# Retention heads one, two and three begin two, two and one slots later in a two-layer mixer kernel

## The chip, the cores and the metric

The kernel runs on one core of a Trainium2 chip. The metric is the device time of one execution in microseconds (us); the times shown are those of whole executions, and the profile comes from one further execution.

## What is computed

The reference is a stack of two layers over 512 positions of width 1024, followed by a norm. A layer normalises x, multiplies it by one wide matrix w_in, and feeds pieces of the result to four branches: a short convolution, a sparse attention (compressed, selected and window parts), a retention and a pooling. Gates weigh the branches, w_o adds them to x, and a gated feed-forward part follows. The change concerns the retention, cut here to what matters:

```
q = rotary(zq, pos, dk); k = rotary(zk, pos, dk) * dk ** -0.5     # 4 heads of 128
def step(R, inp):                                                 # chunks of 128 positions
    scores = einsum('bhnd,bhmd->bhnm', qc, kc) * intra            # decay, causal
    inner  = einsum('bhnm,bhme->bhne', scores, vc)
    ...
mu = mean(o); var = mean(square(o - mu))
o = ((o - mu) * rsqrt(var + EPS)) * gn_g
return o * silu(zg)
```

The kernel does a head as one decayed causal product over the 512 positions, in four row blocks of keys.

## The kernel before, in words

Everything is transposed: features on the 128 partitions, the 512 positions along the free dimension. Every weight matrix is cut into groups of 128 output features by 1024 input features (512 KB). SyncE (SP) loads the groups in order into a ring of three; ScalarE (ACT) copies a group to its high part `w_hi` (L431, two groups ahead of the matmul, once the group before has been multiplied); GpSimd (POOL) subtracts to make the low part `w_lo` in two halves (L415); TensorE (PE) multiplies a group in 24 matmuls of 512 columns (L1107 to L1109: high by high, high by low, low by high, for eight chunks). VectorE (DVE) takes the finished product out of one of two accumulators with the step `take` (L650), which also frees that accumulator; PE may be two products ahead of it at most.

After twelve groups for the attention inputs (A) come 32 groups (B) that make the inputs of retention, convolution and pooling. Their order is the table `B_TILES`: head h of the retention has its four tiles rq, rk, rv, rg at the places 0, 16, 20 and 24 on. Each B product is cut in four quarters of six matmuls, and between the quarters PE does small pieces of the branches. The table `SIDE` says which piece stands in which of the 128 slots (slot n is quarter n mod 4 of product n div 4). PE, DVE and ACT each walk through the same table in order, and each does its own part of every piece, so that a place in the table is a place in three queues. No engine passes a step that waits.

For head h, with n0 = `RET_SLOT[h]`, the loop over the heads puts these pieces:

```
for _m in range(QT):
    SIDE[_n0 + _m].append(("ret_scores", _h, _m))
    SIDE[_n0 + _m + 1].append(("ret_values", _h, _m))
SIDE[_n0 + 5].append(("ret_gate", _h))
SIDE[_n0 + 6].append(("ret_var", _h))
SIDE[_n0 + 7].append(("ret_inverse", _h))
SIDE[RET_SLOT[_h] + (8, 8, 8, 12)[_h]].append(("ret_end", _h))
SIDE[RET_SLOT[_h] + (14, 12, 12, 14)[_h]].append(("ret_split", _h))
SIDE[4 * (RET0[_h] + 3) + 3].append(("ret_turn", _h))
SIDE[4 * (_b + 2) + 1 + _k].append(("rotate", B_TILES[_b], _k))
```

The last two do not depend on `RET_SLOT`: the transposes of rv (`ret_turn`) and the rotary steps (`rotate`) stay by their tiles.

What each piece is:

- `ret_scores` (PE L1316, rk by rq into a bank `s`; DVE L872 multiplies it by the decay into `pr`). Block 0 waits for the rotated rk. `ret_values` (PE L1326, rv by pr into a bank `o`) waits for that multiplication.
- with the last `ret_values` ACT squares and copies the result (L527, L528). `ret_gate`: ACT tanh of rg (L522), DVE L886. `ret_var`: PE L1333 sums the squares over partitions, ACT takes the square root (L532), DVE inverts one half (L892); `ret_inverse`: DVE inverts the other (L895). tanh and root each need a table load on ACT. `ret_end` (DVE L906, L908) scales, `ret_split` (DVE L899, L900) writes the high and low parts.
- `ret_turn`: PE transposes rv_T (L1191, waits for the take of rv), DVE L879, L880.
- `rotate`: ACT issues two DMAs that swap the halves of rq or rk into `rot` (L459, L460), at the start of the product after that tile, when the tile's take is done; DVE L690, L692 in one slot and L694 in the next.
- `pool` (PE L1342, DVE L918, L919), and for ACT a load of the decay table of a head (L498) at products 14, 18, 22 and 26.

On ACT, the start of every B product is in this order: the copy `w_hi`, the two swap DMAs, the decay DMA; the pieces of that product's four slots follow.

After B come eight rounds that multiply gates and branches, the product with w_o, and the feed-forward part; the change touches nothing there.

Of the kernel before, what the change touches and what calls it, by code (L numbers as in the profile page):

```python
# [69 lines left out]
A_TILES = ["k_cmp", "v_cmp", "k_slc", "k_win", "v_slc", "v_win", "q0", "q1", "q2", "q3", "gate", "pad"]  # L70
RET0 = [0, 16, 20, 24]
SC0 = [4, 7, 10, 29]
RET_SLOT = [68, 80, 96, 112]
POOL0 = [28, 13, 14, 15]
POOL_SLOT = [127, 85, 101, 117]
B_TILES = [None] * B_GROUPS
# [29 lines left out]
for _h in range(RH):  # L106
    _n0 = RET_SLOT[_h]
    for _m in range(QT):
# [6 lines left out]
for _h in range(RH):  # L115
# [3 lines that stand above are left out]
# [1429 lines left out]
```

## Time and profile before

| | us |
|---|---|
| median of 3 runs (2152.16 to 2152.82) | 2152.51 |
| the profiled execution | 2152.31 |
| its span, first to last instruction | 2150.5 |
| mean granted TensorE clock over the span | 0.988 of full |
| chain of work that ended last: PE, DVE, issue | 91%, 6%, 2% |
| B slots 80 to 127 of layer 0, about | 310 to 408 |

The page gives the busy time of each engine, the chain of work that ended last (followed back from the last instruction to whatever released each step), and groups of instructions by line. A timeline lists instructions of one engine in order; the bracket at the end is the idle time of the engine just before, and who ended it. An x2 or x4 row stands for as many passes.

### The profile page before, as it was taken

The numbers are of one execution on the slowest core, as the hardware profiler recorded it, in microseconds if no ns is written. First come the engines' busy times: TensorE is split into PE (matmuls) and PEld (weight loads), VectorE is DVE, ScalarE is ACT, GpSimd is POOL, SyncE is SP. The second block draws the span as 40 slices with busy tenths as digits, with TensorE's granted clock in tenths as the row PEclk, the third lists the DMA queues.
The fourth block names the chain that finished last, engine by engine and source line by source line (L and its number), as shares of the span: only waits on it lengthen the run. The fifth ranks groups of instructions, "written<-read, shape, count | busy, mean of one in ns | idle before, by whom it ended". The sixth has DMA issues, their size and how long they took to land.

```text
span 2150.5 us, 32302 instructions
## 1 busy us (share of the span) xinstructions
PE 2086.4 (97%) x9834; PEld 1643.1 (76%) x9834; DVE 1227.3 (57%) x1856; ACT 659.8 (31%) x961; POOL 920.8 (43%) x676
## 2 busy tenths in 40 slices
PE   7999989999999999999999999999999999999997
PEld 5766667788888788888877666668888887888885
DVE  8656766622235888872157568565223278888513
ACT  3244423333332222222223445223233322222222
POOL 3422223444444555545534222234444454555552
PEclk9999999999999999999999999999999999999998
DMA  5311122222222222223232111222322232222332
GB/s 188 103 55 50 50 64 89 85 93 96 98 98 98 88 98 98 98 90 109 98 122 93 50 40 50 77 86 88 102 94 96 98 98 89 97 98 98 101 107 98
DMA packets 57131, 194.90 MB, mean 91 GB/s; under 512 B 6864, under 2 KB 7248, under 8 KB 56912
## 3 DMA queue, kind: packets, MB, share of 16 engines
q1 hardware_dynamic: 52272, 186.14, 26.1%
q10 hardware_dynamic: 4768, 7.61, 1.4%
q8 instruction: 50, 0.82, 0.2%
q14 instruction: 41, 0.34, 0.1%
HBM read 186.64 MB, written 2.10 MB: 88 GB/s over the span
## 4 chain that ended last, share of the span: by engine, by line
PE 91%; DVE 6%; issue 2%; ACT 0%; DMA 0%; DVEq 0%; ACTq 0%; SPq 0%
PE acc L1107 27%; PE acc L1109 27%; PE acc L1108 27%; PE o L1292 2%; PE s L1266 2%; PE t L1274 2%; PE o L1326 1%; PE s L1253 1%; PE s L1316 1%; PE s L1183 0%; PE t L1303 0%; DVE ssq L639 0%; DVE xg_lo L618 0%; PE s L1342 0%; DVE y_lo L900 0%
## 5 line engine op out<-in xcount | busy, mean ns | idle before, releaser
L415 POOL TENSOR_TENSOR w_lo<-w_raw,w_hi 128x512 fp32r<-128x512 f32 x672 | 920.6, 1390 | 1202.1 <-ACT w_hi L431 1190.4
L1107 PE MATMUL acc<-xg_hi,w_hi 128*128 128x512 f32 x1904 | 780.1, 410 | 18.4 <-DVE xg_lo L618 11.5
L1109 PE MATMUL acc<-xg_hi,w_lo 128*128 128x512 f32 x1904 | 748.9, 393 | 0.0
L1108 PE MATMUL acc<-xg_lo,w_hi 128*128 128x512 f32 x1904 | 748.0, 393 | 0.0
L431 ACT ACTIVATE w_hi<-w_raw 128x1024 fp32r<-128x1024 f32 x336 | 355.1, 1057 | 902.0 <-PE acc L1109 837.8
L1107 PEld LDWEIGHTS acc<-xg_hi,w_hi 128*128 128x128 f32 x1904 | 360.8, 190 | 127.3 <-issue 38.8
L1109 PEld LDWEIGHTS acc<-xg_hi,w_lo 128*128 128x128 f32 x1904 | 361.0, 190 | 77.8
L1108 PEld LDWEIGHTS acc<-xg_lo,w_hi 128*128 128x128 f32 x1904 | 361.7, 190 | 76.4 <-issue 6.9
L987 DVE TENSOR_TENSOR work<-acc,rstd 128x512 f32<-128x512 f32 x64 | 44.1, 690 | 256.1 <-PE acc L1109 256.1
L1107 PE MATMUL acc<-act_hi,w_hi 128*128 128x512 f32 x352 | 136.9, 389 | 0.0
L1108 PE MATMUL acc<-act_lo,w_hi 128*128 128x512 f32 x352 | 136.9, 389 | 0.0
L1109 PE MATMUL acc<-act_hi,w_lo 128*128 128x512 f32 x352 | 136.9, 389 | 0.0
L1081 DVE SCALAR_TENSOR_TENSOR x<-acc,x 128x512 f32 x16 | 11.1, 693 | 177.5 <-PE acc L1109 177.5
L993 DVE SCALAR_TENSOR_TENSOR work<-work,acc 128x512 f32<-128x512 f32 x64 | 44.0, 687 | 103.1 <-PE acc L1109 103.1
L1107 PE MATMUL acc<-y_hi,w_hi 128*128 128x512 f32 x256 | 99.6, 389 | 0.0
L1108 PE MATMUL acc<-y_lo,w_hi 128*128 128x512 f32 x256 | 99.6, 389 | 0.0
L1109 PE MATMUL acc<-y_hi,w_lo 128*128 128x512 f32 x256 | 99.6, 389 | 0.0
L566 ACT ACTIVATE work<-work 128x512 f32<-128x512 f32 x44 | 27.8, 632 | 186.4 <-DVE work L1036 186.4
L1108 PEld LDWEIGHTS acc<-act_lo,w_hi 128*128 128x128 f32 x352 | 66.1, 188 | 13.8
L1107 PEld LDWEIGHTS acc<-act_hi,w_hi 128*128 128x128 f32 x352 | 66.1, 188 | 13.7
L1109 PEld LDWEIGHTS acc<-act_hi,w_lo 128*128 128x128 f32 x352 | 66.1, 188 | 13.7
L842 DVE COPY pT<-t 128x128 f32<-128x128 f32 (+3 forms) x128 | 56.8, 486 | 28.3 <-PE t L1274 27.4
(190 smaller groups left out, 2231.1 us busy)
## 6 DMA issues: line engine op xcount, KB each, us to landing
w_raw<-weights_dram SPq DMA_DIRECT2D x339, 512.0 KB, 3.3
x<-xT_dram SPq DMA_DIRECT2D x8, 256.0 KB, 6.1
rot<-rq ACTq DMA_DIRECT2D x16, 128.0 KB
rot<-rk ACTq DMA_DIRECT2D x16, 128.0 KB
dec<-decay_dram ACTq DMA_DIRECT2D x8, 256.0 KB, 3.6
out_dram<-x SPq DMA_DIRECT2D x8, 256.0 KB, 2.2
con<-consts_dram SPq DMA_DIRECT2D x1, 1598.0 KB, 10.8
w1k<-w_dram SPq DMA_DIRECT2D x2, 512.0 KB, 9.3
```

Of the source, the lines that this page charges most:

```text
L415: nc.gpsimd.tensor_tensor(w_lo[:, k, part], w_raw[:, k, part], w_hi[:, k, part].bitcast(F32), ALU.subtract).then_inc(lo_ready, 1)
L431: nc.scalar.activation(w_hi[:, slot, :], w_raw[:, slot, :], ACT.Copy).then_inc(hi_ready, 1)
L566: nc.scalar.activation(work[:, 2, :], work[:, 1, :], ACT.Tanh, scale=0.5).then_inc(silu_ready, 1)
L842: t_end(ve.tensor_copy(pT[:, u % 2, 0:w], t_of(e)[:, 0:w]), e)
L987: ve.tensor_tensor(work[:, n, :], acc[n % 2][:, :], rstd[:, :], ALU.mult).then_inc(acc_free, 1)
L993: ve.scalar_tensor_tensor(out=work[:, n, :], in0=work[:, n, :], scalar=1.0, in1=acc[n % 2][:, :], op0=ALU.add, op1=ALU.mult).then_inc(acc_ ...
L1107: mm(tile, w_h, right_hi, start=first, stop=False)
L1108: mm(tile, w_h, right_lo, start=False, stop=False)
L1109: return mm(tile, w_l, right_hi, start=False, stop=last)
L1266: mm(b[:, 0:w], qT[r, h % 4, qi * P:(qi + 1) * P], kT[r, br, 0:w], start=True, stop=True).then_inc(s_done, 1)
L1274: ins = nc.tensor.transpose(b[:, k * P:(k + 1) * P], pr_of(u)[:, k * P:(k + 1) * P], ident)
L1292: ins = mm(o_bank[qi % 2][d, j * P:(j + 1) * P], v[:, d], p[:, half, :], start=(br == 0 and k == 0), stop=(br == 1 and k == qi + 1))
```

## The change

Heads one, two and three begin at the slots 82, 98 and 113 in place of 80, 96 and 112. All that is counted from `RET_SLOT` moves with them; `ret_turn`, `rotate`, `pool`, the tiles, the DMAs at the start of a product and head zero stay.

```diff
-RET_SLOT = [68, 80, 96, 112]
+RET_SLOT = [68, 82, 98, 113]
```

ACT, between the third and the fourth product after head one's scores (slots 85 to 88), before. L522 is the tanh of the gate, L532 the root, L431 the copy for the next weights, L459 and L460 the swap of rk of head two, L498 the decay of head two:

```order
L522 ACT_TABLE_LOAD
L522 ACTIVATE rg_t<-rg 128x512
L530 REGISTER_ALU
L532 ACT_TABLE_LOAD
L532 ACTIVATE pT<-s,con 128x512
L429 REGISTER_ALU
L430 REGISTER_ALU
L431 ACTIVATE w_hi<-w_raw 128x1024
L455 REGISTER_ALU
L457 REGISTER_ALU
L459 DMA rot<-rk 64x512
L460 DMA rot<-rk 64x512
```

and now:

```order
L522 ACTIVATE rg_t<-rg 128x512
L429 REGISTER_ALU
L430 REGISTER_ALU
L431 ACTIVATE w_hi<-w_raw 128x1024
L455 REGISTER_ALU
L457 REGISTER_ALU
L459 DMA rot<-rk 64x512
L460 DMA rot<-rk 64x512
L497 REGISTER_ALU
L498 DMA dec<-decay_dram 128x512
L530 REGISTER_ALU
L532 ACT_TABLE_LOAD
```

The root (L532, its table load and the activation after it) has moved from before the start of product 22 to behind it: behind the weight copy, the two swap DMAs and the decay DMA. The same holds for head two at product 26. For head three, gate and root stay in one product (29), as before.

DVE from the gate of head one to the take of rk of head two, before (L603 and the like are register work):

```order
L886 SCALAR_TENSOR_TENSOR rg<-rg_t,rg 128x512
L603 REGISTER_ALU
L655 REGISTER_ALU
L918 TENSOR_SCALAR y_hi_58<-s,vec 128x512
L603 REGISTER_ALU
L919 SCALAR_TENSOR_TENSOR y_lo_62<-s,vec,y_hi_58 128x512
L891 REGISTER_ALU
L892 RECIPROCAL pT<-pT 128x256
L603 REGISTER_ALU
L895 RECIPROCAL pT<-pT 128x256
L662 REGISTER_ALU
L649 REGISTER_ALU
```

and now:

```order
L886 SCALAR_TENSOR_TENSOR rg<-rg_t,rg 128x512
L603 REGISTER_ALU
L649 REGISTER_ALU
L650 TENSOR_TENSOR rk<-acc,rstd 128x512
L651 REGISTER_ALU
L891 REGISTER_ALU
L892 RECIPROCAL pT<-pT 128x256
L603 REGISTER_ALU
L895 RECIPROCAL pT<-pT 128x256
L662 REGISTER_ALU
L689 REGISTER_ALU
```

The take of rk (L650) stood behind both reciprocals and stands now before them; the two pool operations have moved ahead of the gate. Both reciprocals are still ahead of the take of rv (L650 further down).

## Rows read from the trace of the kernel before

**Rows 1.** The page, busy time, share of the span and instructions of each engine
```profile
PE 2086.4 (97%) x9834; PEld 1643.1 (76%) x9834; DVE 1227.3 (57%) x1856; ACT 659.8 (31%) x961; POOL 920.8 (43%) x676
```

**Rows 2.** Waits of the matmul engine, whole run: total us, times, longest us
```profile
PE s L1316 <- DVE rk L694: 14.7, 6, 3.5
```

**Rows 3.** Timeline of PE, layer 0, head one: start us, us, engine line op
```profile
309.63 0.63 PE L1191 MATMUL t<-con,rv_T 128*128 128x128 f32 x4 [0.53 <-DVE rv_T L650]
...
315.17 1.12 PE L1316 MATMUL s<-rq,rk 128*128 128x512 f32 x2 [3.53 <-DVE rk L694]
...
319.27 0.81 PE L1316 MATMUL s<-rq,rk 128*128 128x384 f32 x2
```

**Rows 4.** Timeline of DVE, layer 0, the stretch before head one
```profile
308.70 0.69 DVE L650 TENSOR_TENSOR rv_T<-acc,rstd 128x512 f32<-128x512 f32 x1
...
310.31 1.80 DVE L908 SCALAR_TENSOR_TENSOR pT<-pT,rg 128x512 f32<-128x512 f32 x1
312.15 1.63 DVE L690 TENSOR_TENSOR rot<-rot,con 128x512 f32<-128x512 f32 x1
```

**Rows 5.** Timeline of ACT, layer 0, heads one to two
```profile
326.93 0.60 ACT L527 ACTIVATE pT<-o 128x512 f32<-128x512 f32 x1 [1.91 <-PE o L1326]
...
328.03 1.28 ACT L522 ACT_TABLE_LOAD   x1
...
331.27 0.69 ACT L532 ACTIVATE pT<-s,con 128x512 f32<-128x512 f32 x1
...
336.72 0.47 ACTq L459 DMA_DIRECT2D rot<-rk  x1
...
338.63 1.06 ACT L431 ACTIVATE w_hi<-w_raw 128x1024 fp32r<-128x1024 f32 x1 [5.40 <-issue]
```

**Rows 6.** Timeline of DVE, layer 0, heads one to two
```profile
329.99 0.69 DVE L886 SCALAR_TENSOR_TENSOR rg<-rg_t,rg 128x512 f32<-128x512 f32 x1 [4.39 <-ACT rg_t L522]
...
332.26 1.75 DVE L892 RECIPROCAL pT<-pT 128x256 f32<-128x256 f32 x1
...
335.92 0.69 DVE L650 TENSOR_TENSOR rk<-acc,rstd 128x512 f32<-128x512 f32 x1
...
340.29 0.68 DVE L650 TENSOR_TENSOR rv_T<-acc,rstd 128x512 f32<-128x512 f32 x1
```

**Rows 7.** Timeline of PE, layer 0, heads one to two
```profile
325.81 0.38 PE L1326 MATMUL o<-pr,rv 128*128 128x128 f32 x2
...
327.41 1.02 PE L1342 MATMUL s<-pool_early,sc 128*128 128x512 f32 x2
...
334.63 0.39 PE L1107 MATMUL acc<-xg_hi,w_hi 128*128 128x512 f32 x1
...
342.80 0.60 PE L1191 MATMUL t<-con,rv_T 128*128 128x128 f32 x4
...
346.74 1.25 PE L1316 MATMUL s<-rq,rk 128*128 128x512 f32 x2 [1.94 <-DVE rk L694]
```

**Rows 8.** Timeline of PE, layer 0, head three
```profile
379.00 1.10 PE L1316 MATMUL s<-rq,rk 128*128 128x512 f32 x2 [1.92 <-DVE rk L694]
```

**Rows 9.** Timeline of PE, layer 1, heads one, two and three
```profile
1372.39 2.07 PE L1316 MATMUL s<-rq,rk 128*128 128x512 f32 x2 [3.49 <-DVE rk L694]
...
1378.46 0.81 PE L1316 MATMUL s<-rq,rk 128*128 128x384 f32 x2
...
1405.91 1.09 PE L1316 MATMUL s<-rq,rk 128*128 128x512 f32 x2 [1.92 <-DVE rk L694]
...
1437.30 1.10 PE L1316 MATMUL s<-rq,rk 128*128 128x512 f32 x2 [1.92 <-DVE rk L694]
```

**Rows 10.** Windows: PE, PEld, DVE, ACT, POOL busy; granted clock; DMA share; GB/s
```profile
347.00:351.00 4.00, 4.00 (x9) 2.52 (x9) 2.08 (x4) 0.00 (x0) 0.63 (x1) 0.57 0.39 131
1372.00:1378.00 6.00, 5.61 (x10) 3.47 (x11) 2.92 (x5) 0.00 (x0) 0.00 (x0) 0.50 0.20 74
```

**Rows 11.** The page, costliest groups: the low-part subtraction
```profile
L415 POOL TENSOR_TENSOR w_lo<-w_raw,w_hi 128x512 fp32r<-128x512 f32 x672 | 920.6, 1390 | 1202.1 <-ACT w_hi L431 1190.4
```

## The prediction

> **What bounds the kernel now.** I read the page first. PE is busy 97% of the span [rows 1]: its matmuls set the time, and whatever PE waits for adds to it. So the next view is the list of PE's waits. The longest entry there by far is the first scores product of a head (L1316), which waits for the rotated rk (L694 on DVE): six times, 14.7 us in all, 3.5 at most [rows 2]. These are heads one, two and three in both layers, just the three starts that the change moves. The timelines give each: 3.53, 1.94 and 1.92 us in layer 0 [rows 3, 7, 8], 3.49, 1.92 and 1.92 in layer 1 [rows 9]. So DVE sets the pace in this stretch, though it is busy 57% of the span.
>
> The reader should then ask why rk is late. It stands in DVE's queue behind the two reciprocals that end the head before, and these wait for the root on ACT. So one chain runs from a head's first scores to the next head's: last values product, squares, tanh, DVE gate, root, reciprocals, scaling, rotary steps, rk. I follow that chain through the new order, counting from the start of head one's scores.
>
> **Head one: the gain.** Up to the new slot 82 no queue has changed, so rk of head one arrives at the same instant, 315.17. PE meanwhile does two more quarters of the product. A quarter takes 1.36 us: six of them lie between 334.63 and 342.80, 8.17 us [rows 7]. So 2.72 us of the 3.53 are filled, and 0.8 is left. The scores still start at the same instant; the two quarters are what is gained, 2.72 us a layer.
>
> **Head one to head two: what is given back.** Times after the start of head one's scores (315.17), layer 0.
> - Last values product: 10.64 before (325.81). The pool product (327.41, 1.0 us long, about 0.9 before the next can go) stands now ahead of it [rows 7]: 11.5.
> - ACT: the squares can start when that product is done, 0.38 after its start [rows 7], since no swap DMAs stand right before them now. From the first square to the tanh's end, 326.93 to 329.96, is 3.03 [rows 5]. So the tanh ends at 11.5 + 0.4 + 3.0 = 14.9. Before it was 14.8. The earlier take of rq and its DMAs cost nothing: they lie in the wait for those values.
> - Here ACT's order changes. The root used to follow the tanh: its result was there at 331.27 + 0.69 = 331.96, and DVE's first reciprocal began at 332.26 [rows 5, 6], 17.1 on the count. Now ACT goes first through the weight copy (1.06, beside DVE's work), then waits for DVE's gate and the take of rk (two operations of 0.69 with gaps, about 1.5 [rows 6]), reaching 16.5; then issues the two swaps and the decay, 336.72 to 338.63, 1.9 us [rows 5]: 18.4; then the table load and the root, 1.28 and 0.69, 2.0: 20.4. **The reciprocals begin at 20.4 in place of 17.1**; DVE stands still for about 4 us in between.
> - From first reciprocal to the end of the take of rv was 332.26 to 340.97, 8.7 us [rows 6]. The take of rk, 0.8 with its gap, has moved out: 7.9, so 28.3.
> - Beside POOL's subtraction some DVE operations last 1.80 and 1.63 in place of about 0.7 [rows 4], 1.0 more each. Before, none of these fell between the reciprocals and the take of rv in this head. Now product 23 ends on PE at about 24.9, ACT copies until 26.0, and POOL subtracts from 26.1 to 29; DVE is then in L908 and L694 of rq. I take two hits, 2.0 us (bounds 0 and 3): the take of rv is done at 30.3, and PE can go 0.24 later, as from 309.39 to 309.63 [rows 3, 4]: 30.6.
> - PE came to the transposes of rv (L1191, slot 95, unmoved) at 342.80, 27.63 on the count and with no wait, and has two quarters fewer before it now: 24.9. **It waits 5.7 us for the take of rv.** Behind it stand the quarter 96 and all that follows; the second accumulator doesn't help, since PE passes nothing.
> - Then the transposes, 0.4, and three quarters, 4.1: head two's scores at 35.1. rk needs about 3.2 of DVE after the take of rv (five operations of the rotary steps and the split, 0.6 to 0.7 apart), so it is no longer late.
>
> The same leg took 346.74 - 315.17 = 31.57 before [rows 3, 7]. So this one costs 3.5, more than head one gained.
>
> **Head two to head three.** ACT and DVE repeat the same order at product 26. Only two quarters follow the transposes, as head three moves by one slot: 30.6 + 0.4 + 2.7 = 33.7, and rk is ready at 33.7 too; I take 33.8. Before it was 32.26 in layer 0 [rows 7, 8].
>
> **Sum.** Layer 0: 35.1 + 33.8 = 68.9, before 63.83: 5.1 more, less the one quarter (1.36) that PE has behind it at head three's start: +3.7. Layer 1: before, 33.52 and 31.39 [rows 9], 64.91: +4.0, less 1.36: +2.6. The gain of head one lies in these sums already, since its start stays and PE is two quarters further. Both together +6.3. Behind head three I take nothing: its gate and root stay in one product, the mean steps of the last pool tile mix in, and eight rounds with a first product of four gates cover the last split; a wait there of up to 1 us a layer is in the range.
>
> **The clock.** After 1.94 us of waiting in layer 0 and 3.49 in layer 1 PE ran at half rate: granted clock 0.57 over four us and 0.50 over six, the 1.2 GHz level [rows 10]. After 3.53 in layer 0 it did not. Layer 1's stretch lengthened the way from head one's first to second scores to 6.07 us [rows 9], against 4.10 in layer 0 [rows 3]: 1.97 us. The legs from which I reckoned +6.3 hold these old stretches, and the new legs hold none. Now there are four waits of 5.7 us, longer than all of these. I price each between 0 (as after 3.53) and 3 (six us at half rate), and take 1.5, near the 1.97 and a little under it since one of the two longest waits went free: +6.0. A half-rate stretch after the transposes falls on PE's own quarters, where nothing covers it.
>
> The Trainium skill, "TensorE: Matmul & The Clock Gate", section "What's actually happening", says that the throttled clock is the default state and activity releases it. By that rule all four waits would end at half rate, at 1.97 each 7.9, and the sum would be 2 us higher; the 3.53 us wait at full clock speaks against it.
>
> **Predicted:** 2152.3 + 6.3 + 6.0 = 2164.6, against the profiled execution's 2152.31, which is 0.2 under the median: 2164.6.
>
> The Trainium skill, "SBUF — State Buffer", section "SBUF: two separate sides", says that a DVE operation with two SBUF inputs and a GpSimd operation lock each other out for a whole instruction. The mean subtraction lasts 1.39 [rows 11]; at that price eight hits (two in each of four legs) would cost 3 us more than my 1.0 each. The rows show 1.1 and 0.9, and they decide.
>
> **The rivals.**
> - *The plain reading, faster.* The root does not end up later: the chain from scores to rk keeps its length, 31.3 a leg, and only the waits for rk shrink. What decides is the first reciprocal on the count: up to about 18 this holds, at 20 it doesn't. Then 62.6 a layer, -1.2 and -2.3, less 1.36 each: -6.3, 2146. For it: the view of waits shows only rk, 14.7 us, and ACT is idle most of the time. Against it: ACT takes its queue in order, and the new order is plain. 6%.
> - *The delay comes, the rest doesn't.* POOL's hits fall elsewhere and the clock stays up. Legs of 33.1 and 31.8 give +1.1 and 0.0, less 1.36 each: -1.7, 2151; with part of either, up to 2156. 10%.
> - *The delay and the hits, no new half rate:* 2158.6; 20%, on the slower side as the forecast.
> - *Longer half rate* after each of the four waits, 3 each: 2170.6. 8%.
> - My forecast with its surroundings, 56%.
>
> That the change doesn't do what it says is shut out by the order of instructions.
>
> **How the numbers follow.** A measurement of this kernel can tell 0.2%, 4.3 us, from no change. Slower than 2156.8 are the forecast, the two rivals of its side: 84%. Within: 10%. Faster: 6%. The range leaves out the faster rival, the lower part of the second and the top of the last: 2155 to 2170.
>
> **What would show it.** Right: the wait L1316 for rk falls from 14.7 to about 2, and L1191 for the take of rv, 0.53 before head one [rows 3], comes to over 20 in all, four times 5 to 6 before heads two and three. ACT's root of heads one and two comes after the decay DMA, and DVE idles about 4 us before L892. Head one's scores start within 0.5 us of 315.2. From there to head two's is 35 to 37. Wrong: the reciprocals begin under 18 us after head one's scores; L1191 waits less than 3; or the clock stays at 1.00 in all four places, which would leave 2159.

## The result, and the profile after

| | before | after |
|---|---|---|
| median (lowest to highest, executions), us | 2152.66 (2152.16 to 2154.18, 4) | 2171.79 (2171.07 to 2172.37, 4) |
| the profiled execution | 2152.31 | 2172.12 |
| its span | 2150.5 | 2170.3 |
| mean granted TensorE clock | 0.988 | 0.983 |

The ratio is 1.0086, with a 95% interval from 1.0072 to 1.0100: slower, as forecast, but by 19 us and not by 12, and above the range that ended at 2170.

The page of the kernel after, busy time and the chain that ended last. PE's share of the chain is 88% (before 91%), DVE's 8% (before 6%), and POOL's subtraction is as long as in [rows 11]:

```profile
PE 2095.4 (97%) x9834; PEld 1650.9 (76%) x9834; DVE 1223.8 (56%) x1856; ACT 660.9 (30%) x961; POOL 922.1 (42%) x676
...
PE 88%; DVE 8%; issue 3%; ACT 1%; ACTq 1%; DMA 0%; DVEq 0%; SPq 0%
...
L415 POOL TENSOR_TENSOR w_lo<-w_raw,w_hi 128x512 fp32r<-128x512 f32 x672 | 921.9, 1393 | 1221.5 <-ACT w_hi L431 1210.0
```

PE's busy time is 9 us above [rows 1] with the same 9834 matmuls. That much of the loss is no wait at all; it is matmuls that lasted longer.

Waits of PE after (total us, times, longest us). The wait for rk in [rows 2], 14.7 us, has shrunk to 1.6, and the transposes of rv_T wait 22.4 in its place, where head one's 0.53 [rows 3] were all there was in layer 0:

```profile
PE t L1191 <- DVE rv_T L650: 22.4, 6, 5.4
...
PE s L1316 <- DVE rk L694: 1.6, 2, 0.8
PE acc L1107 <- DVE work L987: 1.6, 2, 0.8
```

Timeline of PE after, layer 0, head one to head two (start us, us, engine, line, operation; in the bracket the idle time before it):

```profile
310.82 0.63 PE L1191 MATMUL t<-con,rv_T 128*128 128x128 f32 x4 [0.54 <-DVE rv_T L650]
...
316.38 1.12 PE L1316 MATMUL s<-rq,rk 128*128 128x512 f32 x2 [0.81 <-DVE rk L694]
...
327.88 0.38 PE L1326 MATMUL o<-pr,rv 128*128 128x128 f32 x2
...
346.77 1.11 PE L1191 MATMUL t<-con,rv_T 128*128 128x128 f32 x4 [5.30 <-DVE rv_T L650]
...
348.11 0.63 PE L1108 MATMUL acc<-xg_lo,w_hi 128*128 128x512 f32 x1
...
354.03 1.02 PE L1316 MATMUL s<-rq,rk 128*128 128x512 f32 x2
```

Head one waits 0.81, head two no longer for rk. Between them the transposes wait 5.30, and the matmuls right behind last 0.63 where they last 0.39 elsewhere.

Timeline of ACT after, the same stretch:

```profile
328.30 0.60 ACT L527 ACTIVATE pT<-o 128x512 f32<-128x512 f32 x1 [8.31 <-PE o L1326]
...
331.24 1.05 ACT L431 ACTIVATE w_hi<-w_raw 128x1024 fp32r<-128x1024 f32 x1
332.98 0.47 ACTq L459 DMA_DIRECT2D rot<-rk  x1
...
334.20 0.53 ACTq L498 DMA_DIRECT2D dec<-decay_dram  x1
334.88 1.28 ACT L532 ACT_TABLE_LOAD   x1 [2.60 <-issue]
336.18 0.69 ACT L532 ACTIVATE pT<-s,con 128x512 f32<-128x512 f32 x1
```

Timeline of DVE after, the same stretch:

```profile
331.37 0.69 DVE L886 SCALAR_TENSOR_TENSOR rg<-rg_t,rg 128x512 f32<-128x512 f32 x1 [3.11 <-ACT rg_t L522]
332.18 0.69 DVE L650 TENSOR_TENSOR rk<-acc,rstd 128x512 f32<-128x512 f32 x1
336.90 1.75 DVE L892 RECIPROCAL pT<-pT 128x256 f32<-128x256 f32 x1 [4.02 <-ACT pT L532]
...
342.77 1.67 DVE L908 SCALAR_TENSOR_TENSOR pT<-pT,rg 128x512 f32<-128x512 f32 x1
344.48 1.63 DVE L694 TENSOR_TENSOR rq<-rq,rot 128x512 f32<-128x512 f32 x1
346.04 0.68 DVE L650 TENSOR_TENSOR rv_T<-acc,rstd 128x512 f32<-128x512 f32 x1
```

The root starts at 336.18 and not, as in [rows 5], before the weight copy; DVE stands still for 4.02 and begins its reciprocals at 336.90, which is 20.52 after the first scores (before 17.09, [rows 3, 6]). L908 and L694 last 1.67 and 1.63 in place of 0.69, 0.98 and 0.94 more: these are the two hits beside POOL's subtraction, which runs from 342.63 to 345.56. The take of rv is done at 346.72.

Granted clock after (windows; the columns are those of [rows 10], the clock is the third number from the end):

```profile
345.00:353.00 8.00, 6.23 (x18) 5.07 (x19) 6.71 (x10) 0.00 (x0) 0.56 (x1) 0.57 0.20 67
383.00:387.00 4.00, 3.43 (x11) 2.91 (x12) 3.86 (x7) 0.00 (x0) 0.00 (x0) 0.57 0.40 131
...
1414.00:1421.00 7.00, 5.14 (x15) 4.23 (x16) 6.80 (x10) 0.00 (x0) 0.65 (x1) 0.51 0.24 76
1451.00:1459.00 8.00, 6.68 (x19) 5.28 (x19) 6.26 (x10) 0.00 (x0) 0.12 (x1) 0.57 0.19 66
```

All four waits for rv stand beside a stretch at the 1.2 GHz level. In windows of 1 us, the shares of full clock that are missing add up to 3.41, 1.71, 3.42 and 3.41 us. I call such a stretch a half-rate stretch, and its sum the missing clock.

**The stretches that the change touches.** In each layer I take the stretch from head one's first scores to the first branch product of the eight rounds, and divide it at head two's and three's first scores and at the last pool product (slot 127). A leg is the way from one head's first scores to the next head's. "Rest" is the span less these stretches of both layers; the last column is the median less the same stretches of the one profile.

| profile | layer 0: one to two, two to three, three to pool, pool to rounds | layer 1 | sum | rest | median us | median less sum |
|---|---|---|---|---|---|---|
| before | 31.57, 32.26, 27.69, 22.66 | 33.52, 31.39, 27.69, 22.66 | 229.4 | 1921.1 | 2152.7 | 1923.2 |
| after | 37.65, 34.19, 25.84, 23.76 | 37.29, 35.58, 25.84, 23.76 | 243.9 | 1926.4 | 2171.8 | 1927.9 |
| after, again | 37.66, 34.21, 25.83, 23.76 | 37.26, 35.57, 25.89, 23.79 | 244.0 | 1927.0 | 2170.6 | 1926.7 |
| before, again | 31.56, 32.23, 27.67, 22.67 | 33.51, 31.38, 27.69, 22.66 | 229.4 | 1921.8 | 2153.8 | 1924.4 |
| root first | 31.90, 31.84, 26.63, 23.76 | 31.92, 31.85, 26.62, 23.80 | 228.3 | 1929.4 | 2158.0 | 1929.7 |
| root behind the copy | 33.65, 31.30, 26.63, 23.76 | 33.43, 31.28, 26.65, 23.75 | 230.5 | 1927.9 | 2158.8 | 1928.3 |
| waits filled | 35.06, 33.03, 26.64, 23.76 | 35.06, 33.03, 26.68, 23.75 | 237.0 | 1925.9 | 2162.5 | 1925.5 |
| tail put back | 37.78, 34.24, 25.83, 22.66 | 37.41, 34.07, 25.82, 22.66 | 240.5 | 1919.8 | 2164.1 | 1923.6 |
| head one alone | 33.84, 31.58, 28.53, 22.66 | 33.85, 31.35, 27.69, 22.66 | 232.2 | 1925.3 | 2157.5 | 1925.3 |
| one slot each | 32.54, 33.28, 27.51, 23.79 | 32.59, 32.38, 26.65, 23.75 | 232.5 | 1920.2 | 2157.0 | 1924.5 |
| late split | 31.17, 29.40, 27.68, 22.67 | 31.42, 29.38, 27.65, 22.67 | 222.0 | 1922.0 | 2145.5 | 1923.4 |
| one and late split | 31.35, 29.42, 27.69, 22.66 | 32.11, 30.23, 27.68, 22.66 | 223.8 | 1921.6 | 2148.1 | 1924.3 |
| shift only | 32.29, 31.40, 28.55, 31.05 | 33.30, 31.40, 27.69, 31.05 | 246.7 | 1923.9 | 2172.3 | 1925.6 |

So of the 19.8 us between the two profiled spans, 14.5 lie in the touched stretches, and 5.3 do not. The two need different explanations.

Behind head three, timeline of DVE after, layer 0, slot 127 and on:

```profile
415.12 0.75 DVE L918 TENSOR_SCALAR y_hi<-s,vec 128x512 fp32r<-128x512 f32 x1 [0.97 <-PE s L1342]
415.90 0.75 DVE L919 SCALAR_TENSOR_TENSOR y_lo<-s,vec,y_hi 128x512 fp32r<-128x512 f32 x1
416.57 0.42 DVE L899 CAST y_hi<-pT 128x512 fp32r<-128x512 f32 x1
417.02 1.66 DVE L900 TENSOR_TENSOR y_lo<-pT,y_hi 128x512 fp32r<-128x512 f32 x1
```

Head three's split (14 slots on, now in slot 127) stands behind the last pool product. DVE waits 0.97 for PE with the split ready to run, and does it afterwards.

### The profile page after: what moved, and what is told of

Read it like the earlier page. It is cut to its first block, busy times and chain, and to the rows that moved or that the text cites. A ratio compares the mean times of both kernels' runs of the same rounds, so it can differ in the third digit from the quotient of the medians.

```text
span 2170.3 us, 32304 instructions
## 1 busy us (share of the span) xinstructions
PE 2095.4 (97%) x9834; PEld 1650.9 (76%) x9834; DVE 1223.8 (56%) x1856; ACT 660.9 (30%) x961; POOL 922.1 (42%) x676
## 4 chain that ended last, share of the span: by engine, by line
PE 88%; DVE 8%; issue 3%; ACT 1%; ACTq 1%; DMA 0%; DVEq 0%; SPq 0%
PE acc L1107 26%; PE acc L1109 26%; PE acc L1108 26%; PE o L1292 2%; PE s L1266 2%; PE t L1274 2%; PE o L1326 1%; PE s L1253 1%; DVE pT L892 1%; PE s L1316 1%; DVE pT L895 0%; DVE pT L908 0%; PE s L1183 0%; PE t L1303 0%; DVE ssq L639 0%
## 5 line engine op out<-in xcount | busy, mean ns | idle before, releaser
L431 ACT ACTIVATE w_hi<-w_raw 128x1024 fp32r<-128x1024 f32 x336 | 355.5, 1058 | 885.3 <-PE acc L1109 837.1
L987 DVE TENSOR_TENSOR work<-acc,rstd 128x512 f32<-128x512 f32 x64 | 44.1, 690 | 254.7 <-PE acc L1109 254.4
```

The lines of the kernel that those rows point to most:

```text
L431: nc.scalar.activation(w_hi[:, slot, :], w_raw[:, slot, :], ACT.Copy).then_inc(hi_ready, 1)
L987: ve.tensor_tensor(work[:, n, :], acc[n % 2][:, :], rstd[:, :], ALU.mult).then_inc(acc_free, 1)
```

## The experiments

The theory: the root's place in ACT's queue delays the reciprocals, DVE's queue carries that to the take of rv, PE waits there, and the clock falls behind the wait. Rivals were that the root is innocent, that the wait costs and the clock does not, and that the loss outside comes from where the work lies in time.

### Root first

From the kernel after, the root is moved ahead of the weight copy in those products whose first slot holds `ret_var`; every slot stays. `ret_root` holds the wait and the activation of the root as they were.

```diff
...
+for e in SIDE[4 * b]:
+    if e[0] == "ret_var":
+        ret_root(e)
 ahead(L, A_GROUPS + b)
...
-elif e[0] == "ret_var":
+elif e[0] == "ret_var" and n % 4:
```

> The changed kernel, but ScalarE takes the root of heads one and two ahead of the weight copy, the swaps and the decay load of products 22 and 26; nothing else moves. Theory (the root's place in ScalarE's queue costs the time): VectorE's first reciprocal begins 16.5 us after the head's first scores in place of 20.5, the wait of the rv transposes (L1191) falls from 5.3 to 1 to 2 us, the half-rate stretches there go, and the legs from head to head come to 31 to 32 us in place of 37.65 and 34.19: 2145 to 2152 us. Rival (VectorE's backlog alone, whatever ScalarE's order): the first reciprocal moves, but the take of rv stays where it was, 30.4 us after the scores, and the time stays at 2172. Second rival (the moved heads cost by lost clock alone): the waits stay above 4 us and only the clock changes.

Measured: 2158.0 (2154.26 to 2162.18, 10 executions), ratio to the kernel before 1.0019 [1.0009, 1.0028]. Waits of PE; the added lines move these numbers by six, so L1197 is the transposes of rv and L1322 the first scores:

```profile
PE t L1197 <- DVE rv_T L656: 8.1, 6, 1.8
PE s L1322 <- DVE rk L700: 5.7, 6, 1.7
```

Timelines of ACT, then of DVE; head one's scores began at 319.18 here:

```profile
335.44 0.69 ACT L491 ACTIVATE pT<-s,con 128x512 f32<-128x512 f32 x1
335.77 0.47 ACTq L459 DMA_DIRECT2D rot<-rk  x1
336.02 1.05 ACT L431 ACTIVATE w_hi<-w_raw 128x1024 fp32r<-128x1024 f32 x1
```

```profile
336.16 1.75 DVE L898 RECIPROCAL pT<-pT 128x256 f32<-128x256 f32 x1 [0.49 <-ACT pT L491]
```

With nothing moved but the root, the first reciprocal comes at 16.98 in place of 20.52, the longest wait for rv falls from 5.4 to 1.8, no half rate stands in the four places, and the touched stretches fall from 243.9 to 228.3. The root alone takes off 15.6, more than the 14.5 that the change had put there, though the 1.1 a layer ahead of the rounds (below) is still in. So the root's place is shown to cause the long waits and the half rate behind them.

But this kernel doesn't beat the one before. The legs came out as I had reckoned; the time did not, and is 6 us above the range expected, because the rest is 8.3 us above that of before. Of these 8.3, 7.1 is missing clock, and 3.4 of that lies ahead of head one's first scores in layer 0, where both kernels do the same work. And the reader should see why the touched stretches gain only 1.1 over before, though head one's wait is 2.7 shorter and 4.7 of missing clock that before has in them is gone: DVE's queue from one scores to the next is as long as ever, and PE waits for it in two places (8.1 and 5.7) in place of one.

### Root behind the copy

The same, with the root behind the weight copy and ahead of the swaps: the three DMA issues by themselves.

> The changed kernel with ScalarE's root of heads one and two behind the weight copy of products 22 and 26, but ahead of the swaps and the decay load. Theory (each step put ahead of the root costs its own time): the first reciprocal begins 18.0 us after the head's first scores, between 17.0 (root first) and 20.5 (root last); L1191 waits 2.5 to 3.5 us, the first leg 33 to 34 us without half rate; 2157 to 2165. Rival (the swaps are what matters, by the memory traffic they start, and not the queue): the reciprocal begins at 18, but the take of rv is as early as with the root first.

Measured: 2158.75 (2154.74 to 2160.14, 10), ratio 1.0022 [1.0013, 1.0031]. Waits of PE, then the timeline of ACT:

```profile
PE t L1197 <- DVE rv_T L656: 10.2, 6, 2.3
```

```profile
332.42 1.04 ACT L431 ACTIVATE w_hi<-w_raw 128x1024 fp32r<-128x1024 f32 x1
333.48 1.28 ACT L491 ACT_TABLE_LOAD   x1
...
334.78 0.69 ACT L491 ACTIVATE pT<-s,con 128x512 f32<-128x512 f32 x1
```

The reciprocals begin 18.03 after head one's scores and the longest wait for rv is 2.3, a little under the 2.5 to 3.5 expected. A half-rate stretch (1.71 missing) stands behind the first of these waits all the same, and two more lie in the legs of layer 1; the expectation had none. So of the 3.5 us by which the root is late, the weight copy makes 1.05 (16.98 to 18.03) and the DMA issues, with the wait for the gate and the take of rk ahead of them, 2.5 (18.03 to 20.52). The take of rv ends 26.8, 27.4 and 30.3 after the scores in the three kernels: the reciprocals carry it.

### Waits filled

From the kernel after: while PE waits for rv of heads two and three, it multiplies 22 times into the transposes' bank, which nobody reads; then the transposes overwrite it.

```diff
+if e[1] >= 2:
+    g = A_GROUPS + RET0[e[1]] + 4
+    group_here(g)
+    pe.wait_ge(t_free, 1 + L * len(T_USES) + T_USES.index(e))
+    last_wait()
+    for _ in range(FILL):
+        mm(t_of(e)[:, :], w_hi[:, g % RING, 0:P], xg_hi[:, 0, :], start=True, stop=True)
...
+FILL = 22
```

> The changed kernel, with 22 matmuls of 512 columns that nobody reads put on TensorE ahead of each of the four long waits for the take of rv (22 by 0.228 is 5.0 us of the 5.3 us wait). It does more work and leaves the wait itself alone. Theory (the waits also cost by the clock that they lose): granted clock 1.00 in all four places, the way from the rv transposes to the next head's scores falls from 7.26 and 4.65 us in layer 0 to 4.5 and 3.2, and from 6.92 and 6.04 in layer 1 likewise; sum 9.5 us: 2162 us. Rival (the half-rate stretches are no cost of their own, since VectorE or ScalarE holds the next step up as well): 2170 to 2172 us, with the clock at full rate.

Measured: 2162.47 (2159.52 to 2164.64, 5), ratio 1.0040 [1.0025, 1.0054]. Window over the first of the four waits, then the timeline of PE there (L1313 is the added matmul; the view begins behind the first two of the 22):

```profile
345.00:353.00 8.00, 7.62 (x36) 6.08 (x35) 7.70 (x10) 1.06 (x1) 2.98 (x2) 1.00 0.38 132
```

```profile
345.62 4.70 PE L1313 MATMUL t<-xg_hi,w_hi 128*128 128x512 f32 x20
350.69 0.66 PE L1191 MATMUL t<-con,rv_T 128*128 128x128 f32 x4 [0.38 <-DVE rv_T L650]
...
351.42 0.39 PE L1108 MATMUL acc<-xg_lo,w_hi 128*128 128x512 f32 x1
```

The transposes come at 30.44 after head one's scores, as in the kernel after (30.39): the wait is as long. Only the clock differs, 1.00 in place of 0.57, and the matmuls behind last 0.39 again. The four legs sum to 136.2 in place of 144.7. **The half rate behind the four waits costs 8.5 us**; 0.8 us a layer of it is given back behind head three, where the way to the last pool product is 26.6 and not 25.8. There DVE had caught up while PE ran slowly: with the waits filled, head three's first values product waits 0.50 for `pr`, and in the kernel after it doesn't wait. Up to the rounds the half rate costs 6.9.

### Tail put back

From the kernel after, head three's end and split stand where they stood before the change.

```diff
-    SIDE[RET_SLOT[_h] + (8, 8, 8, 12)[_h]].append(("ret_end", _h))
-    SIDE[RET_SLOT[_h] + (14, 12, 12, 14)[_h]].append(("ret_split", _h))
+    SIDE[RET_SLOT[_h] + (8, 8, 8, 11)[_h]].append(("ret_end", _h))
+    SIDE[RET_SLOT[_h] + (14, 12, 12, 13)[_h]].append(("ret_split", _h))
```

> The changed kernel, but scaling and split of head three stay at their old slots 124 and 126 (11 and 13 after its start in place of 12 and 14). Theory (the split of head three behind the last pool product makes VectorE late for the gate rounds after it): the wait for the first take of the gate rounds (L987, twice 0.8 us) goes, and the way from the last pool product to the first branch product is 22.7 us in place of 23.8, in both layers: 2.2 us less, 2169.6 us. Rival (VectorE is late there from the mean steps and the reciprocals, whatever the split): no change, 2171.8 us.

Measured: 2164.1 (2160.85 to 2177.63, 7), ratio 1.0071 [1.0047, 1.0095]. Timeline of DVE, layer 0, slot 126 and on:

```profile
413.67 0.43 DVE L899 CAST y_hi<-pT 128x512 fp32r<-128x512 f32 x1
414.12 0.69 DVE L900 TENSOR_TENSOR y_lo<-pT,y_hi 128x512 fp32r<-128x512 f32 x1
414.94 0.75 DVE L918 TENSOR_SCALAR y_hi<-s,vec 128x512 fp32r<-128x512 f32 x1
```

The split is done before the pool product's turn, the way to the rounds is 22.66 again in both layers, and the wait for L987 is gone: the 1.1 us a layer is the split's place. The time fell by more than those 2.2, to 5.5 under what I had expected. Its executions lie in two clusters, 2160.9 to 2164.1 (four) and 2173.3 to 2177.6 (three), and the profile is of the lower. In it the leg from head two to three in layer 1 is 1.5 shorter than after (a half-rate stretch lost 1.71 there and not 3.41) and the rest is 6.6 shorter. So the median says little on the tail, and the leg says it.

### Head one alone; one slot each

Both edits are shown against the kernel after.

```diff
-RET_SLOT = [68, 82, 98, 113]
+RET_SLOT = [68, 82, 96, 112]
```

> The kernel before with head one alone two slots later (82), heads two and three at 96 and 112. Theory (the root of the head that moves by two goes behind the start of the next product): the take of rv of head two is 30.4 us after head one's scores, L1191 waits 5.4 there and nowhere else, with half rate behind it; the leg from head one to two is 33.5 to 34.5 us, from two to three 31.4 as before; 2 to 5 us slower than before: 2154 to 2158. Rival (the cost comes from heads two and three being late against their tiles, not from head one): 2147 to 2150, since head one's 2.7 us a layer are gained.

Measured: 2157.5 (2153.24 to 2167.19, 10), ratio 1.0018 [1.0004, 1.0033]. Waits of PE:

```profile
PE t L1191 <- DVE rv_T L650: 11.7, 4, 5.3
...
PE s L1316 <- DVE rk L694: 5.5, 4, 2.0
```

Each head pays for its own move: only the transposes of head two wait 5.3 now, and head three starts as before. The leg from one to two is 3.8 shorter than in the kernel after, by the two quarters that no longer stand behind the transposes and ran partly at half rate.

```diff
-RET_SLOT = [68, 82, 98, 113]
+RET_SLOT = [68, 81, 97, 113]
```

> The kernel before with heads one, two and three each one slot later (81, 97, 113). The root of heads one and two then stays in its old product, ahead of the weight copy and the swaps. Theory (two slots are too many because of the root, one is not): ScalarE's root follows the tanh, the first reciprocal begins about 17.1 us after the scores, L1191 waits under 1.5 us, the waits for rk are near 2 us in all six places, the legs are 31.4 to 32.5; no half rate behind head one. The time is that of before within 3 us: 2150 to 2155. Rival (any shift against the fixed tiles costs, in proportion): half of what the change cost, 2160 to 2164.

Measured: 2156.97 (2153.02 to 2160.97, 10), ratio 1.0019 [1.0009, 1.0028]. Waits of PE:

```profile
PE s L1316 <- DVE rk L694: 12.6, 6, 2.2
...
PE t L1191 <- DVE rv_T L650: 3.7, 6, 0.7
```

At 81 the root stays in the product of the gate, and the first reciprocal comes 16.24 after head one's scores; the wait of 5.3 needs the second slot. There is no gain over before either; the time is 2 us above the range expected and 3 below the rival's. The waits for rk went from 3.5, 1.9, 1.9 to some 2.1 each: the wait is moved from one head to another, since the chain between them is as long as before.

### Late split; one slot and late split

If DVE's queue is what bounds a leg, then work taken out from ahead of rk must shorten it. From the kernel before, the split of heads one and two moves out of the slot in which it stands between the take of rv and the rotary steps of rk.

```diff
-    SIDE[RET_SLOT[_h] + (14, 12, 12, 14)[_h]].append(("ret_split", _h))
+    SIDE[RET_SLOT[_h] + (14, 16, 16, 14)[_h]].append(("ret_split", _h))
```

> The kernel before, starts unchanged, but the split of heads one and two (L899, L900, 0.8 and 1.66 us on VectorE ahead of the next head's rk) comes 16 slots after the head's start in place of 12, behind the next head's first scores. Theory (VectorE's queue between root and rk sets the legs, and only its length counts): rk is ready 1.9 to 2.5 us earlier, the waits of L1316 for heads two and three fall from 1.9 to 0, the legs from 31.5 to 29.5 us; 8 us faster: 2143 to 2147. Rival (rk has other things to wait for, and the waits move to L1191 or L1326): 2151 to 2153.

Measured: 2145.47 (2143.92 to 2145.83, 5), ratio 0.9960 [0.9946, 0.9974]. It beats both kernels. Waits of PE, the timeline of DVE, and a window around head one, here and then in the kernel before:

```profile
PE s L1316 <- DVE rk L694: 7.0, 2, 3.5
```

```profile
344.49 0.69 DVE L690 TENSOR_TENSOR rot<-rot,con 128x512 f32<-128x512 f32 x1 [0.42 <-DMA rot<-rk]
345.10 1.77 DVE L692 TENSOR_TENSOR rk<-rk,con 128x512 f32<-128x512 f32 x1
346.91 0.69 DVE L694 TENSOR_TENSOR rk<-rk,rot 128x512 f32<-128x512 f32 x1
```

```profile
315.00:322.00 7.00, 5.33 (x10) 3.20 (x11) 4.16 (x7) 0.00 (x0) 0.00 (x0) 0.51 0.23 75
```

```profile
315.00:322.00 7.00, 6.16 (x21) 3.85 (x22) 3.25 (x6) 0.00 (x0) 0.00 (x0) 1.00 0.15 58
```

The waits for rk of heads two and three are gone, the leg from two to three is 29.4 in place of 32.3 and 31.4, and 7.4 us go from the touched stretches. DVE now waits 0.42 for the swap DMA, so that transfer is the next thing to be late. Head one's wait of 3.5 is left, in both layers now with a half-rate stretch behind it.

The next thought is to shorten that wait too. From the kernel before, with the late split: head one at slot 81, its split at 96 still.

> The kernel before with head one alone one slot later (81) and the splits of heads one and two behind the next head's first scores (slot 96 and 112). Theory (rk sets the starts; one slot leaves the root in its product and shortens the 3.5 us wait that costs half rate): head one's wait for rk 2.2 us with no half rate behind it, heads two and three none to 0.7; legs 29.5 to 30.5, 29.4; 1 to 4 us under the late split alone (2145.5): 2141 to 2144. Rival (half rate behind head one's wait is not tied to its length): same as the late split alone, 2144 to 2146.

Measured: 2148.14 (2147.20 to 2152.81, 11), ratio 0.9979 [0.9970, 0.9988]: no better than the late split alone, and 4 us above the range expected. The wait for rk is 8.8 in four pieces, 2.2 at most, so head two has begun to wait again.

### Shift only; both kernels again

The 5.3 us outside could come from everything behind layer 0's B lying later in time. So the kernel before gets 37 unread matmuls a layer, at full rate 8.4 us, ahead of the eight rounds.

```diff
+group_here(J0)
+pe.wait_ge(t_free, 2 + (L + 1) * len(T_USES))
+for _ in range(37):
+    mm(t_bank[0][:, :], w_hi[:, J0 % RING, 0:P], xg_hi[:, 0, :], start=True, stop=True)
```

> The kernel before, all steps in place, with 37 matmuls of 512 columns that nobody reads between the last B slot and the gate rounds, in both layers: 8.4 us each of work without a wait, the amount by which the changed kernel is late there in layer 0. It adds 16.9 us of its own. Theory (half rate outside the changed stretches depends on the instant at which the later work comes): low clock shows near 728, 1110 to 1118 and 1209 to 1217 us as in the changed kernel, and the time is 2172 to 2176. Rival (it comes from the order or the waits in the changed stretch): the old places, only shifted, and 2152.7 + 16.9 = 2169 to 2171.

Measured: 2172.3 (2172.0 to 2174.28, 4), ratio 1.0091 [1.0076, 1.0107]. The added matmuls are 16.8 us (31.05 - 22.66, twice), the rest is 2.8 above that of before. Half-rate stretches do move (318 to 323, 1383 to 1391), but not to where the kernel after has its own, 727 to 732 and 1209 to 1217. So a later time alone doesn't reproduce the changed kernel. Nor can the later time be what moved them all: the stretches 182 to 190, 233 to 241 and 318 to 323 lie ahead of the first added matmul, where before has 101 to 106 and 183 to 188 and none near 240 or 320, though both kernels have done the same instructions up to there.

> The changed kernel once more, unchanged. Its profile showed 14.5 us more than before in the stretches from head one's scores to the gate rounds, both layers, and 5.3 us more elsewhere, where half-rate stretches of 1.7 us lost clock each lie at other places. Theory (where these fall elsewhere is a matter of the execution): the 243.9 us of the changed stretches come again within 2 us, the rest does not: single executions between 2164 and 2174, and the rest of the span between 1919 and 1930. Rival (the change shifts the later work so that half rate comes there every time): all executions within 1 us of 2171.8.

Measured: 2170.62 (2169.08 to 2172.83, 5), ratio 1.0080 [1.0066, 1.0093]. The legs agree with the first profile within 0.05, the rest within 0.6, and all twelve half-rate stretches lie in the same places to 1 us. I had expected the rest not to come again.

> The kernel before once more. Theory: the same stretches as in its first profile, 229.4 us from head one's scores to the gate rounds in both layers and 1921 us for the rest, each within 3 us; its half-rate stretches behind heads one and two may move, the waits may not. Rival (its profile was a lucky one): the rest comes to 1925 or more.

Measured: 2153.79 (2152.10 to 2158.30, 8), ratio 1.0004 [0.9994, 1.0014]. The same holds for before: legs within 0.04, rest within 0.7. So the extra 5 us of the rest belong to the changed kernel and aren't an accident of one profile.

## Why the prediction was right and wrong

**What held.** Count from head one's scores, layer 0.

| step | predicted | measured |
|---|---|---|
| wait for rk of head one | 0.8 | 0.81 |
| last values product | 11.5 | 11.50 |
| the tanh's end | 14.9 | 14.95 |
| first reciprocal | 20.4 | 20.52 |
| DVE still before it | about 4 | 4.02 |
| operations hit by POOL | two, 1.0 each | two, L908 and L694, 0.98 and 0.94 |
| the transposes of rv | 30.6 | 30.39 |
| PE's wait there | 5.7 | 5.30 |

The sign and the mechanism are right, and root first shows that the order on ACT is the cause of the long waits in these stretches. Two of the prediction's additions are 0.1 or 0.2 off by its own terms: 14.9 and 1.5 make 16.4, and rk of head three would be ready at 33.5 (30.3 and 3.2). Neither moves the forecast.

**Two markers missed.** The way from head one's scores to head two's was 37.65 and not 35 to 37; with the waits filled it is 35.06, so the excess is the half rate. And head one's scores began at 316.38 and not within 0.5 of 315.2. The cause lies before the change: the transposes of head one were 1.19 later already (310.82, [rows 3] has 309.63), and the wait for rk was as said. Up to there the two kernels do the same, and 8.5 us of clock are missing in both; why this one is later is not known.

**The steps that failed are two terms put at nothing and one sized too small.** The largest: **the sum had nothing for the rest of the program**, which is 5.3 us longer. The second: "Behind head three I take nothing", which measured 1.1 a layer, 2.2 us. The third is **the clock term**, "I price each between 0 and 3, and take 1.5: +6.0". Waits filled measured it at 8.5 for the four, 2.1 each. I had taken less than the 1.97 of layer 1's old stretch because one long wait had gone free, which treated the four as one average chance; all four fell in fact, and the other figure that the prediction gives, 7.9 for all four, was nearer. That "nothing covers it" was wrong as well: 1.6 us came back behind head three, so that up to the rounds the clock cost 6.9, only 0.9 above the term. The clock term by itself would have left the time inside the range; the two terms at nothing took it out.

The account against the forecast of +12.3, by profiled executions:

| | us |
|---|---|
| four legs without half rate: 136.2 (waits filled), predicted 137.8 | -1.6 |
| half rate behind the four waits: 8.5, predicted 6.0 | +2.5 |
| head three to the last pool product: -1.85 a layer, predicted -1.36 | -1.0 |
| last pool product to the rounds: +1.1 a layer, predicted 0 | +2.2 |
| rest of the program: predicted 0 | +5.3 |
| sum (7.4 by the rows, 0.1 of rounding) | +7.5 |

The second and third rows belong together: with the clock at its net 6.9 they read +0.9 and +0.6. The legs without half rate are a little shorter than I said, by the second of each layer (33.03 in place of 33.8): head two doesn't wait for `pr` as head one does, its last values product comes at 10.6 on its count and not at 11.5, and the transposes at 29.5, where I had carried head one's 30.6 over. The tail is what I had put in the range as "up to 1 us a layer" and left out of the sum. It could be read from the table: head three's split moves from slot 126 to 127 (113 and 14), where the last pool product stands ahead of it; the tail put back shows this to be its cause.

**The rest: what it costs is shown, why it comes is open.** Outside the touched stretches, the kernel after has a half-rate stretch at 727 to 732 that before doesn't have (1.70 lost), and two of before's, 1101 to 1106 and 1241 to 1246 with 1.70 and 1.71, have become 1110 to 1118 and 1209 to 1217 with 3.42 each. Counted over the whole run but its end, before loses 18.8 us of clock and after 30.7: 12 more, of which the four waits' own are 12.0 less the 5.1 that the stretches 347 to 351 and 1371 to 1379 had taken before, so 6.8, and 5.1 lie elsewhere.

The profiles together show that this clock is the cost. Of the 5.3 us, 4.7 lie between layer 0's first branch product and head one's first scores of layer 1 (943.0 before, 947.7 after), 1.2 lie ahead of layer 0's head one, and the end is 0.5 shorter. No edit changes the work of that middle part, in any of the 13 profiles (where head one starts later, PE does one or two more quarters in what was its wait). Its length goes from 941.5 to 947.8 and the clock missing in it from 3.4 to 10.2, but the length less the missing clock is 937.2 to 938.3 in every one. So the 4.7 are missing clock (5.5 before, 10.2 after).

Why more clock is missing there in the kernel after was not found. The later time alone doesn't make it (shift only), and it doesn't need the waits for rv (root first has only short ones, and the rest is 8 us more than before). By the last column of the first table it is 1927 to 1930 in after, after again, root first and root behind the copy, and 1923 to 1926 in all others, two of which have the same `RET_SLOT` as these. My range had no room for it.

**The rivals.** The plain reading is out: the reciprocals began at 20.5. "The delay comes, the rest doesn't" is out: the two hits came, and the clock fell. "No new half rate", 2158.6, is out. The filled waits come nearest to it: 2162.5, 3.9 above it, of which 4.8 is the rest of that profile over before's. "Longer half rate", 2170.6, came nearest in time, yet not for its reason, 3 us behind each wait (2.1 was measured); that it came near is chance.

## What to carry to other kernels

When an edit shifts a step across the start of a block of queued work, compare each engine's order of instructions first: two slots later on PE cost nothing there, but put a root behind a copy and three DMA issues on ACT, and another engine's queue paid for it. A wait that comes from a chain as long as the interval it must fit moves with the edit and doesn't go; what removes it is to take work out of that chain, as the late split did by moving four small operations. And where each new wait on TensorE may drop the clock, allow for the drop, and for several us in places that the edit doesn't touch.

## What the hardware showed that I hadn't expected

- **The length of the wait doesn't decide the clock.** A wait of 3.53 for rk of head one was followed by a clock of 1.00 in the kernel before, and one of 3.52 in the same place by 0.51 with the late split (window 315 to 322). The 1.94 us wait of [rows 7] had 0.57 behind it [rows 10]. All four waits of about 5.3 were followed by the 1.2 GHz level. That the throttled clock is the default and activity releases it, as "TensorE: Matmul & The Clock Gate" of the Trainium skill, section "What's actually happening", says, agrees with these four; it doesn't tell the 3.53 that stayed at full clock from the 1.94 that did not.
- **The loss comes in two sizes.** In all the profiles, a half-rate stretch loses about 1.70 or about 3.41 us of clock (1.69 to 1.71, 3.41 to 3.42), the stretch at the run's end apart.
- **The places are a kernel's own.** Two profiles of the same kernel, taken at different times, have them in the same places to 1 us, and small edits move them, far from the edit too, and even ahead of it, where the instructions done so far are the same. So when two kernels differ by a few us, compare the missing clock outside the edit first: between before and after it was 5 us that no step of the edit explains.
- **Matmuls that nobody reads can pay.** 22 of them in each of four waits made the changed kernel 9 us faster (2162.5 against 2171.8).
